# Gate builds in two rounded matmuls a token, with the low rows on GpSimd and a loop of two bodies

## The reference, cut to what matters

```python
def peer_ffn(h, w_query, sub_keys, expert_u, expert_v):
    ...
    idx = jnp.take_along_axis(cand_i, pos, axis=-1)      # 128 of 16384 experts a token
    gate = jax.nn.softmax(top_s, axis=-1)
    ...
        u = jnp.take(expert_u, ii, axis=0)
        a = jnp.einsum('ted,td->te', u, xi)
        w = gi * jax.nn.gelu(a, approximate=False)
        vv = jnp.take(expert_v, ii, axis=0)
        return jnp.einsum('te,ted->td', w, vv)
```

## Time and profile before

| | us |
|---|---|
| median of 3 runs | 1617.86 |
| lowest, highest | 1613.93, 1621.97 |
| the profiled execution | 1612.43 |
| its span | 1610.3 |
| granted TensorE clock, mean share | 0.991 |
| busy: TensorE / VectorE / ScalarE / GpSimd | 1552.8 / 1224.9 / 703.5 / 428.6 |

### The profile page before, as it was taken

One profiled execution on the slowest core, in us unless ns is written; L12 is line 12 of the kernel. 1 busy time (PEld: TensorE's weight loads), 2 busy tenths in 40 slices (PEclk: granted clock), 3 DMA queues, 4 the chain that ended last, 5 costly groups with the idle time before them and its releaser, 6 DMA issues.

```text
span 1610.3 us, 22989 instructions
## 1 busy us (share of the span) xinstructions
PE 1552.8 (96%) x7813; PEld 1324.4 (82%) x7813; DVE 1224.9 (76%) x2225; ACT 703.5 (44%) x1289; POOL 428.6 (27%) x326
## 2 busy tenths in 40 slices
PE   5999889999899999999999999999999999999996
PEld 5777755545499999999989999998888888888885
DVE  5788633398469888898789976558888888888888
ACT  3532533213368733785348843333333333333333
POOL 1004200001034400243004444313344433344320
PEclk9999999999999999999999999999999999999998
DMA  8964700001269975699648999969999999999992
GB/s 320 335 236 143 288 0 0 1 1 53 71 224 372 366 258 187 247 360 358 224 162 313 363 391 394 410 221 347 345 341 364 357 356 333 358 358 361 341 325 92
DMA packets 173076, 425.77 MB, mean 264 GB/s; under 512 B 13372, under 2 KB 62524, under 8 KB 169800
## 3 DMA queue, kind: packets, MB, share of 16 engines
q1 hardware_dynamic: 86704, 265.37, 44.2%
q0 software_dynamic: 36864, 134.23, 23.4%
q10 hardware_dynamic: 49432, 25.19, 5.5%
HBM read 372.32 MB, written 52.43 MB: 264 GB/s over the span
## 4 chain that ended last, share of the span: by engine, by line
PE 86%; DMA 5%; DVE 5%; issue 1%; ACT 1%; POOL 1%; SPq 0%; DVEq 0%; ACTq 0%
PE bank L1256 10%; PE bank L1258 10%; PE bank L1257 10%; PE bank L1311 10%; PE bank L1315 10%; PE bank L1312 10%; PE bank L1200 7%; PE bank L1271 5%; PE bank L1183 3%; DMA weights<-gates_dense 2%; DMA weights<-in_w_ada 1%; PE bank L1210 1%; PE bank L1118 1%; PE bank L1122 1%; PE bank L1119 1%
## 5 line engine op out<-in xcount | busy, mean ns | idle before, releaser
L1256 PE MATMUL bank<-h_hi,u_hi 128*128 128x384 f32 x1024 | 348.8, 341 | 5.8 <-DVE h_lo L1689 4.3
L1257 PE MATMUL bank<-h_lo,u_hi 128*128 128x384 f32 x1024 | 343.8, 336 | 0.0
L1258 PE MATMUL bank<-h_hi,u_lo 128*128 128x384 f32 x1024 | 343.8, 336 | 0.0
L1311 PE MATMUL bank<-v_hi,w_hi 128*128 128x512 f32 x768 | 299.1, 389 | 0.6 <-DVE w_lo L1797 0.6
L1312 PE MATMUL bank<-v_lo,w_hi 128*128 128x512 f32 x768 | 298.8, 389 | 0.0
L974 ACT ACTIVATE v_hi<-weights 128x1024 fp32r<-128x1024 f32 x128 | 135.8, 1061 | 329.6 <-PE bank L1315 275.5
L1695 DVE TENSOR_TENSOR u_lo<-weights,u_hi 128x1024 fp32r<-128x1024 f32 x128 | 156.5, 1222 | 112.3 <-PE bank L1258 94.3
L1315 PE MATMUL bank<-v_hi,w_lo 128*128 128x512 f32 x768 | 236.5, 389 | 0.0
L1793 DVE TENSOR_TENSOR v_lo<-weights,v_hi 128x1024 fp32r<-128x1024 f32 x128 | 157.6, 1231 | 92.1 <-ACT v_hi L974 91.9
L1256 PEld LDWEIGHTS bank<-h_hi,u_hi 128*128 128x128 f32 x1024 | 193.8, 189 | 7.4 <-issue 4.5
L1257 PEld LDWEIGHTS bank<-h_lo,u_hi 128*128 128x128 f32 x1024 | 193.9, 189 | 0.0
(11 more groups left out here) (293 smaller groups left out, 2277.6 us busy)
## 6 DMA issues: line engine op xcount, KB each, us to landing
weights<-in_uT SPq DMA_DIRECT2D x128, 512.0 KB, 5.9
weights<-in_expert_v SPq DMA_DIRECT2D x128, 512.0 KB, 6.2
gates_dense<-weights SPq DMA_DIRECT2D x24, 1024.0 KB, 7.5
weights<-gates_dense ACTq DMA_DIRECT2D x16, 1536.0 KB, 26.9
shared<-gelu_dense SPq DMA_DIRECT2D x64, 384.0 KB, 7.4
shared<-in_w_ada SPq DMA_DIRECT2D x16, 1024.0 KB, 5.3
gelu_dense<-weights SPq DMA_DIRECT2D x32, 384.0 KB, 5.9
gelu_dense<-ada SPq DMA_DIRECT2D x32, 384.0 KB, 5.2
```

The lines of the kernel that those rows point to most:

```text
L1256: nc.tensor.matmul(a, uh[:, k, :], h2_hi[:, :, k, :], start=(k == 0), stop=False)
L1257: nc.tensor.matmul(a, uh[:, k, :], h2_lo[:, :, k, :], start=False, stop=False)
L1258: ins = nc.tensor.matmul(a, ul[:, k, :], h2_hi[:, :, k, :], start=False, stop=(k == KC - 1))
L1311: nc.tensor.matmul(acc, wh, v_hi[:, r % 2, cols], start=begin, stop=False)
```

## The change

- **Builds.** ScalarE makes a rounded copy of the turned gates (`gate_hi`); GpSimd subtracts it from the gates (`low_gates`), which leaves the low gates. For a half ScalarE writes rounded rows x `gate_hi` to a buffer of its own, `hot_hi`; GpSimd multiplies the same one-hot rows by the low gates in one instruction of 128x1024 into `hot_lo` (`low_rows`). A token's matrix is two float32r matmuls of 128 columns that add up in the bank, with the same loaded operand. `hot_hi` and `hot_lo` have two buffers each and wait for earlier builds.
- **Products.** `products_behind`: of three halves, one has two products behind it. 16 products come into the halves, so the loop has bodies 14 and 15 only.
- **Dots.** 90 lie behind the halves (before: 84), 10 in the selections, 28 in the loop.
- **GpSimd's order** is written out: low rows and gathers of `expert_u` in turn.
- **End of the loop.** The final Gelu, its multiply and the memset (`sparse_weights`) stand behind VectorE's first step of the second part, and the gate loads at (14, 0) and (15, 2).

```diff
-LOOP_AT = 12
+LOOP_AT = 14
+DOTS_IN_CHUNKS = 90
+DOTS_AT_LOOP = (2, 2, 2, 1) * 4
+G_LOADS_AT = {(14, 0): 0, (15, 2): 1}
+def products_behind(half):
+    return 2 if half % 3 == 2 else 1
...
+            def low_rows(half):
+                pool.wait_ge(hot_made, half + 1)
+                if half >= HALVES:
+                    pool.wait_ge(built, (half - 1) * HTOK // BATCH)
+                at = half % (P // HTOK) * HTOK
+                low = turned[:, half * HTOK // P % 2, 2, at:at + HTOK]
+                nc.gpsimd.tensor_tensor(hot_lo[:, half % HALVES], hot[:, half % HALVES, 0].bitcast(F32),
+                                        low.unsqueeze(2).broadcast_to([P, HTOK, P]), ALU.mult).then_inc(hot_lo_made, 1)
...
+                low_gates(d)
+                for h in range(HALVES):
+                    low_rows(d * P // HTOK + h)
+                for h in range(HALVES * d * CHUNKS, HALVES * (d + 1) * CHUNKS):
+                    if h + HALVES < HALVES * (d + 1) * CHUNKS:
+                        low_rows(h + HALVES)
+                    gathers_behind_dots()
+                    dots += sum(dots_behind(h))
...
                 for q in range(HTOK):
                     token = half % (P // HTOK) * HTOK + q
-                    rows = hot_i[:, half % HALVES, q, :]
-                    ins = nc.scalar.activation(rows, rows, ACT.Copy, scale=turned[:, half * HTOK // P % 2, 2, token:token + 1])
+                    ins = nc.scalar.activation(hot_hi[:, half % HALVES, q, :], hot[:, half % HALVES, 0, q, :].bitcast(F32), ACT.Copy,
+                                               scale=gate_hi[:, token:token + 1].bitcast(F32))
...
+                pe.wait_ge(hot_lo_made, half + 1)
...
-                        ins = nc.tensor.matmul(bank[6 + batch % 2][:, q * P:(q + 1) * P], hot_j[:, half % HALVES, b * BATCH + q, :],
-                                               hot_i[:, half % HALVES, b * BATCH + q, :], start=True, stop=True)
+                        token, to = b * BATCH + q, bank[6 + batch % 2][:, q * P:(q + 1) * P]
+                        second = hot[:, half % HALVES, 1, token, :]
+                        nc.tensor.matmul(to, second, hot_hi[:, half % HALVES, token, :], start=True, stop=False)
+                        ins = nc.tensor.matmul(to, second, hot_lo[:, half % HALVES, token, :], start=False, stop=True)
```

More of the change, by code:

```diff
@@ L68, with dots_behind @@
 BEFORE_TURN, AFTER_TURN = 1, 2
-LOOP_AT = 12
-DOTS_BESIDE = (4, 3)
+LOOP_AT = 14
+DOTS_IN_CHUNKS = 90
 DOTS_AT_SEGMENTS = (2, 5, 8, 11, 14)
-DOTS_PER_BODY = {12: 12, 13: 12, 14: 10}
-FEW_DOTS_AT = 14
-G_LOADS_AT = {(13, 0): 0, (15, 0): 1}
+DOTS_AT_LOOP = (2, 2, 2, 1) * 4
+G_LOADS_AT = {(14, 0): 0, (15, 2): 1}
+def products_behind(half):
+    return 2 if half % 3 == 2 else 1
+def dots_behind(half):
+    total = DENSE * P // HTOK
+    dots = DOTS_IN_CHUNKS * (half + 1) // total - DOTS_IN_CHUNKS * half // total
+    behind = products_behind(half)
+    return [dots * (i + 1) // behind - dots * i // behind for i in range(behind)]
 FULL_ROWS, SHORT_ROW = 3, 4
@@ L537, in load_a @@
                     .then_inc(a_in[b], 16)
-            with sp.Fori(LOOP_AT, FEW_DOTS_AT) as I:
-                for r in range(BODY):
-                    loop_product(I, r, True)
             wait_full(sp, "turn", DENSE - 1)
+            sp.wait_ge(built, DTOK // BATCH)
             for b in range(2):
@@ L638, in _, with stage, gather_u, gather_v @@
             pool.wait_ge(iota_made, 2)
-            def gather_rows(table, which, used):
+            def stage(n):
+                first = n // STAGED * STAGED
+                nc.gpsimd.tensor_copy(idx_slot[:, n // STAGED % 2, :], idx[:, 0, first:first + STAGED]).then_inc(idx_staged, 1)
+                pool.wait_ge(idx_staged, n // STAGED + 1)
+            def gather_u(n):
+                if n % STAGED == 0:
+                    stage(n)
+                if n >= ROWS:
+                    pool.wait_ge(dot_done, n - ROWS + 1)
+                pool.sem_inc(granted, 1)
+                nc.gpsimd.indirect_dma_start(ring(n % ROWS), None, expert_u,
+                                             bass.IndirectOffsetOnAxis(idx_slot[:, n // STAGED % 2, n % STAGED:n % STAGED + 1], 0))\
+                    .then_inc(gathered[n % ROWS], 16)
+            def gather_v():
                 def one_round(i, half, first):
@@ L940, in _ @@
                         gate_rows(h + HALVES)
+                    for _ in range(products_behind(h) - 1):
+                        product(m)
+                        m += 1
             def loop_product(I, r, more):
@@ L993, in _ @@
             gelu(ITERS - 1, BODY - 1)
+            act.wait_ge(dot_done, NSEL)
+            nc.scalar.activation(act_w[:, :], act_w[:, :], ACT.Gelu).then_inc(gelu_done, 1)
             for r in range(1, BODY):
@@ L1294, in _ @@
                     build(h)
-                    product(m)
-                    m += 1
+                    for _ in range(products_behind(h)):
+                        product(m)
+                        m += 1
             with pe.Fori(LOOP_AT, ITERS) as I:
@@ L1750, in _ @@
                         hot_rows(h + HALVES)
-                    product(m)
-                    m += 1
-                    for _ in range(DOTS_BESIDE[h // 2 % 2] // 2 + (h % 2 and DOTS_BESIDE[h // 2 % 2] % 2)):
-                        next_dot()
+                    for beside in dots_behind(h):
+                        product(m)
+                        m += 1
+                        for _ in range(beside):
+                            next_dot()
             def loop_product(I, r):
```

86 lines of the change are left out of this document (56 added, 30 removed).

## The result

| | before | after |
|---|---|---|
| median, us | 1617.9 | 1660.6 |
| lowest, highest | 1613.9, 1622.0 | 1659.2, 1663.4 |
| profiled execution, its span | 1612.4, 1610.3 | 1659.2, 1657.0 |
| granted TensorE clock, mean | 0.991 | 0.985 |

Measured side by side, the changed kernel takes 1.0271 times as long, with a 95% interval of 1.0254 to 1.0288: slower by 44 us (the two medians are 42.7 us apart). The forecast was 1654.

What follows compares the result with a forecast made beforehand. TensorE's own work was taken to bound the kernel before, VectorE in slots with low rows after. 30 + 4 + 1 + 1.7 = +36.7 us on 1612.4 gives 1649, forecast as a median of 1654; range 1608 to 1698.

Steps and rivals of the forecast that it cites:

- Builds: TensorE's 16 build instructions a half: 105 to 111 ns each, 1.68 to 1.78 us a half, no gain.
- rival 1: In 48 slots (a half plus its products), no exclusion and short matmuls at streaming pace: faster, say 1592 us; chance 0.10.
- Four products behind three halves: Moving 16 products from the loop into the halves: 4.16 us each in either place, so 0 alone.
- Low rows: GpSimd's multiply costs VectorE 2.15 us; its slot becomes 8.04 us, 0.71 over TensorE's, in 42 slots: +30 us.
- The turn: Ahead of each tile's halves: VectorE has 11.0 us of work against two products' 8.3; +4 us in all.
- ScalarE and the gathers: Build slots: ScalarE's 5.1 us stays under TensorE's 7.33, and gathers issued one slot late land in time; 0.
- Loop: Loop of 16 products: 29 to 31 MB need 70 to 75 us against 66.6; 0 to +8, taken as +1.
- Four u buffers and the ring hide most: In the loop: buffering hides most of the transfer time above TensorE's 66.6 us, leaving 0 to +8 us.
- Hand-over: From loop to second part: VectorE's chain ends at 1077.6, TensorE's first step at 1075.9; +1.7 us.
- Rival 2: No exclusion, builds as dear as now: TensorE stays the bound at 7.33 us a slot; 1621 us, chance 0.12.
- Rival 3: GpSimd's low-row instruction dearer, 3.0 us with nothing overlapped: +84 us, 1702; upper end of the main case (0.78).
- The signs: Expected in a build stretch: TensorE well under 95% busy, VectorE near 100%, some VectorE instructions of 3 us, 8.0 us slots.

Runs made afterwards that it cites:

- e4b: e1b with the two rounded build matmuls of a token streaming 64 of their 128 columns: 1629.5 us.
- e1b: Changed kernel with GpSimd's multiply for the low rows replaced by clearing memsets, so the gates' low part is left out: 1627.4 us.
- e6: Changed kernel's schedule alone: plain float32 builds, rows gated in place by ScalarE, GpSimd only gathers: 1629.1 us.
- e5: Changed kernel with only the dots moved: one behind a one-product half, three or four behind a two-product half: 1641.6 us.
- e2: Changed kernel with GpSimd's multiply replaced by two memsets of the same buffer, which write SBUF and read nothing: 1627.2 us.
- e9: e8 with 14 of the loop's 28 dots, and their gathers, moved behind the halves: 1623.6 us.
- e11: e1b with one rounded build matmul of 256 columns a token in place of two of 128, gate matrices wrong: 1596.7 us.
- e8: Changed kernel with the low rows made by ScalarE instead of GpSimd, same output: 1635.0 us.

## Why the prediction was right, point by point

The side, the size (1654 for 1660.6) and the mechanism were right: VectorE and GpSimd take turns, the low part of u comes late, and TensorE waits for it. The closeness of the number is in part luck, since terms inside the sum were wrong and made up for each other.

- **Builds: no gain.** Right: 0.11 us an instruction, at the top of my 105 to 111 ns. What decided was to take the row of 64-column matmuls and not the difference between 512 and 384 columns. That row is of plain float32 matmuls, each of them two instructions, so it was no sure guide to rounded ones; e4b then showed rounded ones at the same cost, with 64 columns as with 128. The difference of 53 ns for 128 columns, on which rival 1 rested, is seen between 256 and 384 columns (0.119 to 0.173 us) and not below. The Trainium skill's page "TensorE: Matmul & The Clock Gate", section "Weight-path perf modes — Fast Weight Load (FWL) and DoubleRow", ties the fast load to weights that are not FP32; no run here shows one for rounded float32.
- **Four products behind three halves: 0.** Right in the stretches where VectorE is undisturbed: e1b and e6 hold 110.2 and 110.0 us. But the move was not free, as e6 shows with 12 us; they come in the loop, see there.
- **Low rows: +30, measured +28.** The term is right by two errors that cancel, and that is luck. What a turn costs was put too high: VectorE loses 1.69 us and not 2.15. GpSimd's multiply takes 2.0 to 2.07 us or 2.8, 2.4 in the mean and so near the 2.46, but the part beyond 2.07 is its own wait for VectorE. VectorE's slot is then 5.89 + 1.69 = 7.58 us, 0.25 over TensorE's, or 42 x 0.25 = 10.5 us, close to the 9.2 that e5 leaves. The other 19 were in no term. The step that failed is the mean over slots: it treats two slots of 5.96 us and one of 10.1 as three of 7.33, which needs an engine that can work ahead by more than the order lets VectorE. VectorE has up to 7.3 us to do where TensorE has 5.96; there TensorE never waits, since its own work had been made ready, and the debt falls due in the next two-product slot. Some 4.7 of the 19 is the clock.
- The Trainium skill's page "SBUF — State Buffer", section "Who interferes with whom", names this exclusion between a VectorE instruction with two SBUF inputs and a GpSimd instruction that reads. The runs agree in kind, and e2 in that writes alone don't do it; the multiplies of 2.8 us agree in that either engine can be the one that waits. By the letter, a whole instruction lost, it would be 2.07 us; measured is 1.69, 82% of it.
- **The turn: +4.** Not seen. From the start of a tile's last build to that of the next tile's first it is 99.0 and 98.8 us, 99.2 and 98.9 before, and the first two-product slot doesn't wait (10.1 us). Only +1.6 is left ahead of the first tile. The +4 makes up for a part of the 11 us by which the loop was put too low.
- **ScalarE and the gathers: 0.** Right. GpSimd's issue of a gather grew from 1.4 to 1.9 us in the mean, but VectorE's dots never waited in a stretch.
- **Loop: 0 to +8, taken +1; measured +12.1.** Wrong, outside its bounds. The bytes were about right (29 to 31 MB; 31.8 moved; by the shapes named, 20 gathers would make it 27) and so was the rate (414 GB/s; 403). Their quotient, 70 to 75 us, was the better forecast of the loop's 78.7, and the step that failed is "Four u buffers and the ring hide most". They hide only what is loaded ahead, and a gather waits for its ring row's dot, as a block waits for its buffer; the stretch before the loop moved only 286 GB/s, so that little more can have been ahead than the buffers hold. e9 shows the cure: dots, and with them gathers, moved forward.
- **Hand-over: +1.7.** Right. TensorE's first steps of the second part in the changed kernel:

```profile
1114.92 0.47 PE L1391 MATMUL bank<-v_hi,w_hi 128*128 128x512 f32 x1 [0.58 <-DVE w_lo L1879]
...
1120.46 0.47 PE L1391 MATMUL bank<-v_hi,w_hi 128*128 128x512 f32 x1 [1.18 <-DVE w_lo L1879]
```

  0.58 + 1.18 = 1.8 us of waits, +2.2 by the difference of the starts.
- **Rivals.** Rival 2 (no exclusion, builds as dear) is e1b and e2: 1627, where its sum gave 1621; the loop is the difference. Rival 1 failed on both of its conditions. Rival 3's 3.0 us with nothing overlapped is not seen: the instruction takes 2.4 in the mean and costs 1.69.
- **The signs.** Of what the prediction wanted to see, TensorE is busy for 95% of a stretch, with idle time ended by the low part of u, VectorE has instructions of 2.9 us among those of 1.22, and a slot is 7.95 us in the mean (119.2 / 15), for 8.0. VectorE is busy for only 92% of the first stretch and not near 100%: it falls behind in the short slots, and behind four of the five long ones it stands 1.1 to 3.9 us for TensorE's build.

What stays open: the 2.4 us in the second part were read, not tested; what took e5's loop to 82.2 us is not known; and the 1.69 us was measured for this one size of multiply.

## What to carry to other kernels

Before giving a second engine half of a job, ask what the first engine's neighbours read meanwhile: the same low rows cost 33 us on GpSimd and 8 on ScalarE (1635.0 - 1627.4), though neither engine was full. Average an engine's load only over as much work as its buffers let it run ahead; else compare slot by slot. Here the layout alone was worth 19 us (e5). And when a loop is shortened by taking TensorE's work out of it, divide its bytes by its new time first: what buffers hide is only what can be loaded earlier.

## What the runs showed of the hardware

- A rounded matmul with weights of its own costs 0.11 us for 64 and for 128 columns (e4b, e1b), 0.12 for 256 (e11) and 0.17 for 384 (4.16 / 24): splitting a plain 128-column matmul into two rounded ones is a wash (110.0 against 110.2 us a stretch).
- GpSimd's multiply of 128x1024 with a repeated operand takes 2.0 to 2.07 us, less than two of 128x512 (1.23 each), or 2.8 where it begins early in a VectorE instruction, and takes 1.69 us from the two-operand VectorE instruction behind; two writes of 0.96 us on GpSimd take nothing (e2), nor do ScalarE's reads (2294 ns, e8).
- Transfers held 402 to 408 GB/s over 20 us windows, at a DMA share of 1.04, while TensorE waited for them.
- In the first tile a wait of 2.0 us (TensorE busy for 3.3 of 5 us) was followed by a granted clock of 0.66 over the next 5 us, and each tile had one such fall; behind waits of the same length at 561, 749 and 962 us the clock stayed at 1.00. In e5, whose waits in the stretches are 1.4 us at the most, it stayed at 1.00 in the same place.
